# Attention of a two-layer transformer kernel: steps taken in pairs on TensorE, with four probability buffers in place of three

## What is computed

```python
def dense_block_attention(q, k, v):            # layer 0
    s = jnp.einsum("bqhgd,bkhd->bhgqk", qblk, k).astype(jnp.float32) * scale
    p = jax.nn.softmax(s, axis=-1).astype(v.dtype)
    return jnp.einsum("bhgqk,bkhd->bqhgd", p, v)

def window_sink_attention(q, k, v, kc, vc, sink):   # layer 1
    s_loc = jnp.where(valid, s_loc, -jnp.inf)  # |i - j| <= WINDOW
    p = jax.nn.softmax(jnp.concatenate([s_loc, s_ctx, s_sink], axis=-1), axis=-1)
    return einsum(p[..., :band], vb) + einsum(p[..., band:band + s_ctx_len], vc)
```

## Time and profile before

| what | value |
|---|---|
| median of 3 runs | 1504.19 us (1504.17 to 1505.51) |
| span of the profiled execution | 1502.7 us |
| TensorE (PE) busy | 1476.1 us, 98% |
| VectorE (DVE) busy | 989.5 us, 66% |
| ScalarE (ACT) busy | 706.6 us, 47% |
| GpSimd (POOL) busy | 667.3 us, 44% |
| mean granted TensorE clock | 0.999 |
| chain that ended last | PE 73% of the span, ACT 2%, issue 2%, DVE 1% |

### The profile page before, as it was taken

One profiled execution on the slowest core, in us unless ns is written; L12 is line 12 of the kernel. 1 busy time (PEld: TensorE's weight loads), 2 busy tenths in 40 slices (PEclk: granted clock), 3 DMA queues, 4 the chain that ended last, 5 costly groups with the idle time before them and its releaser, 6 DMA issues.

```text
span 1502.7 us, 26249 instructions
## 1 busy us (share of the span) xinstructions
PE 1476.1 (98%) x10198; PEld 1268.9 (84%) x10198; DVE 989.5 (66%) x1500; ACT 706.6 (47%) x1229; POOL 667.3 (44%) x447
## 2 busy tenths in 40 slices
PE   6999999999999999999999999999999999999997
PEld 4888874578999989999899999865579998999997
DVE  5899877579778556476667655766634655456464
ACT  4645326762733424334243544355536454445365
POOL 0031026602656334353435433355645756556463
PEclk9999999999999999999999999999999999999999
DMA  9532110045224142244546211200012423224222
GB/s 374 215 129 99 44 43 1 2 174 184 93 90 149 64 138 93 64 163 150 186 139 216 94 59 57 74 26 1 1 57 99 126 71 127 85 84 142 93 91 84
DMA packets 51674, 157.04 MB, mean 105 GB/s; under 512 B 5568, under 2 KB 13120, under 8 KB 50016
## 3 DMA queue, kind: packets, MB, share of 16 engines
q1 hardware_dynamic: 51120, 155.17, 30.0%
q0 software_dynamic: 432, 0.20, 0.1%
HBM read 153.38 MB, written 2.10 MB: 103 GB/s over the span
## 4 chain that ended last, share of the span: by engine, by line
PE 73%; ACT 2%; issue 2%; DVE 1%; POOL 0%; DVEq 0%; ACTq 0%
PE psum L3449 31%; PE psum L3476 13%; PE psum L3482 7%; PE psum L2862 6%; PE psum L3408 4%; PE psum L3134 3%; PE psum L3421 2%; PE psum L2938 2%; PE psum L3102 1%; PE psum L3032 1%; DVE product L1924 1%; PE psum L3119 1%; PE psum L3104 1%; PE psum L3106 1%; PE psum L3108 1%
## 5 line engine op out<-in xcount | busy, mean ns | idle before, releaser
L1181 POOL TENSOR_TENSOR flow<-fraw,fhi 128x512 fp32r<-128x512 f32 x168 | 232.8, 1405 | 100.2 <-ACT fhi L1629 90.7
L1629 ACT ACTIVATE fhi<-fraw 128x512 fp32r<-128x512 f32 (+1 forms) x272 | 163.3, 614 | 164.6 <-DMA fraw<-weights_dram 103.1
L3476 PE MATMUL psum<-gated,fhi 128*128 128x512 f32 (+1 forms) x1032 | 217.7, 355 | 0.0
L2862 PE MATMUL psum<-act,whi 128*128 128x512 f32 (+1 forms) x1008 | 215.5, 332 | 0.1
L1187 POOL TENSOR_TENSOR flow<-fraw,fhi 128x512 fp32r<-128x512 f32 (+1 forms) x96 | 125.9, 1331 | 180.5 <-ACT fhi L1629 179.9
L3476 PEld LDWEIGHTS psum<-gated,fhi 128*128 128x128 f32 x1032 | 169.2, 188 | 28.8 <-issue 0.3
L3449 PE MATMUL psum<-tlo,fhi 128*128 128x384 f32 (+1 forms) x608 | 187.9, 309 | 0.0
L3449 PE MATMUL psum<-thi,fhi 128*128 128x384 f32 (+1 forms) x608 | 187.8, 309 | 0.0
L2862 PEld LDWEIGHTS psum<-act,whi 128*128 128x128 f32 x1008 | 154.0, 189 | 20.8 <-issue 2.3
L2565 DVE SCALAR_TENSOR_TENSOR xT<-psum,mod,xT 128x512 f32<-128x512 f32 (+1 forms) x141 | 87.5, 654 | 95.8 <-PE psum L3482 95.8
L3449 PE MATMUL psum<-bhi,fhi 128*128 128x384 f32 (+1 forms) x456 | 140.6, 308 | 0.1
(11 more groups left out here) (293 smaller groups left out, 3340.4 us busy)
## 6 DMA issues: line engine op xcount, KB each, us to landing
fraw<-weights_dram SPq DMA_DIRECT2D x88, 512.0 KB, 3.8
adr_late<-adat_dram SPq DMA_DIRECT2D x49, 512.0 KB, 3.6
raw<-weights_dram SPq DMA_DIRECT2D x44, 512.0 KB, 3.4
fraw<-weights_dram SPq DMA_DIRECT2D x64, 256.0 KB, 2.8
adr<-adat_dram SPq DMA_DIRECT2D x26, 512.0 KB, 4.6
ada_w<-ada_dram SPq DMA_DIRECT2D x8, 1024.0 KB, 13.9
fraw<-weights_dram SPq DMA_DIRECT2D x32, 192.0 KB, 2.5
xT<-x_in_dram SPq DMA_DIRECT2D x3, 1024.0 KB, 16.8
```

Source lines behind the costliest of these rows:

```text
L1181: nc.gpsimd.tensor_tensor(low_piece(L, j, x), weight_piece(L, j, x), high_piece(L, j, x).bitcast(F32), ALU.subtract).then_inc(sem("f_lo"), 1)
L1629: A(high_piece(L, j, x)[:, 0:cols], source, ACT.Copy).then_inc(sem("f_hi"), 1)
L2862: last = MM(out_[:, o:o + t1 - t0], w_, a_[:, t0:t1], start=k == order[0] and j == 0, stop=k == order[-1] and j == 2)
L3476: MM(ps, wh_, a_[:, t0:t1], start=k == 0 and i == 0, stop=False)
```

## The change

TensorE takes two steps at a time: the scores of the next two steps, then the values of this step and the next. A piece of maxima stands before the two scores and another behind them. Sums, `rows` and the work of ACT move behind pairs; the first pair of scores stands ahead of the loop. `probT` becomes four separate buffers, the fourth of them in the place of the rope tables (`O_CON`), so the fourth exponential waits for the last rope. The pieces of layer 1 change their order and their places; the last piece of unit 1, now masked, is made in the last projection block. In layer 0 the first scores wait for both last projection blocks, and `rows(0, 1)` stands ahead of the loop.

```diff
-NPT = 3
+NPT = 4
...
-            units.append(dict(j=j, q0=0, nq=NX, slots=3, pieces=[far[0], ends, near[0], near[1], far[1]],
+            units.append(dict(j=j, q0=0, nq=NX, slots=3, pieces=[far[0], near[0], ends, far[1], near[1]],
...
 def pieces_beside(layer, i, a):
-    units = UNITS[layer]
+    n = len(UNITS[layer])
     if layer == 1:
-        n, p = (i + 1, 4) if a == 0 else (i + 2, a - 2)
-        return [], [(n, p)] if n < len(units) and p >= 0 and (n, p) != (1, 4) else []
+        p = {0: 0, 1: 1, 3: 2, 4: 3, 5: 4}.get(a)
+        return [(i + 2, p)] if p is not None and i + 2 < n else []
     if i % 2 == 0:
-        return [], [(i + 2, 0)] if a == 1 and i + 2 < len(units) else []
-    return [], [(i + 2, a)] if i + 2 < len(units) else []
-
-def rows_at(layer, i):
-    return layer
+        return [(i + 2 + a, 0)] if i + 2 < n else []
+    return [(i + 2, a + 1)] if i + 2 < n and a < 5 else []
+
+def rows_behind(layer, i, a):
+    n = len(UNITS[layer])
+    if layer == 1:
+        return i + 1 if a == 0 and i + 1 < n else None
+    u = i + 1 if a == 0 else i + 2
+    return u if i % 2 and a in (0, 4) and u < n else None
...
+                    if t == NPT - 1:
+                        act.wait_ge(*na("rope", L, 5 if L == 0 else 9))
...
+                def behind_short(i):
+                    if i + 1 < len(units):
+                        minus_top(0, i + 1)
+                    if i >= 2:
+                        out_high(i - 2)
+
+                def behind_long(i, a):
+                    heads = [(*divmod(i // 2, 2), *divmod(n, 2)) for n in range(4)]
+                    if a == 1:
+                        if i >= 2:
+                            inverse(i - 2)
+                        given_by_heads(*heads[0])
+                    if a == 3:
+                        if i >= 2:
+                            out_high(i - 2)
+                        given_by_heads(*heads[1])
+                        if i + 1 < len(units):
+                            minus_top(0, i + 1)
+                        inverse(i - 1)
+                        given_by_heads(*heads[2])
+                    if a == 5:
+                        given_by_heads(*heads[3])
+
+                def behind_windowed(i, a):
+                    if a == 1 and queries_at(1, i) is not None:
+                        q_high(1, queries_at(1, i))
+                    if a == 3:
+                        if i + 1 < len(units):
+                            minus_top(1, i + 1)
+                        if i >= 1:
+                            inverse(i - 1)
+                    if a == 5:
+                        if i + 1 < len(units):
+                            sink_share(1, i + 1)
+                        if i >= 1:
+                            out_high(i - 1)
...
                 for i, u in enumerate(units):
-                    for a in range(len(u["steps"])):
+                    for a in range(0, len(u["steps"]), 2):
                         exponential(i, a)
+                        exponential(i, a + 1)
...
                     for a in range(len(u["steps"])):
                         if a == 0 and i >= 1:
                             evacuate(i - 1)
-                        if L == 0 and short and a == 0 and i >= 2 or L == 0 and not short and a == 0 and i + 1 < len(units):
-                            top(0, i + 1)
-                        if L == 0 and short and a == 0 and i >= 2:
-                            outputs(i - 2)
-                        if L == 0 and not short and a == 1 and i >= 2:
+                        if L == 0 and i >= 2 and a == (0 if short else 1):
                             outputs(i - 2)
...
-                        if L == 0 and short and a == 1 and i >= 2:
+                        if L == 0 and i >= 2 and a == (1 if short else 3):
                             out_low(i - 2)
-                        for pieces in pieces_beside(L, i, a):
-                            taken(L, pieces, a)
+                        taken(L, pieces_beside(L, i, a))
...
-                        if a == 1 and i >= 1:
+                        if a == 2 and i >= 1 or a == 1 and short and i >= 1:
                             denominators(i - 1)
-                        if L == 1 and a == 4 and i >= 1:
+                        if L == 1 and a == 5 and i >= 1:
                             out_low(i - 1)
...
             def maxima(L, i, p):
...
-                if piece_banks(L, i, p)[0] == 0 and i >= 1:
-                    pe.wait_ge(*na("neg", L, i if L == 1 or i % 2 == 0 else i - 1))
+                if L == 1 and i >= 2:
+                    pe.wait_ge(*na("neg", 1, i - 1 if p < 2 else i))
...
             def rows(L, i):
...
+                if L == 1 and 1 <= i and i + 1 < len(U[1]):
+                    pe.wait_ge(*na("mx", 1, U[1][i + 1]["m0"] + 2))
-                if L == 0 and i == 1:
-                    pe.wait_ge(*ev(FIRST[("out", 0)] - 1))
-                if L == 0 and i > 2 and i % 2 == 0:
+                if L == 0 and i >= 1:
+                    pe.wait_ge(*na("neg", 0, i))
+                if L == 0 and i > 2:
                     pe.wait_ge(*na("fln", 0, i - 2))
...
             def attention(L):
...
-                if L == 0:
-                    pe.wait_ge(*ev(FIRST[("out", 0)] - 2))
-                else:
-                    for n in range(2):
-                        pe.wait_ge(*ev(FIRST[("out", 1)] - 2 + n))
+                for n in range(2):
+                    pe.wait_ge(*ev(FIRST[("out", L)] - 2 + n))
                 order = steps_of(L)
                 scores(0, 0)
-                scores_masked(0, 0)
-                for t, (i, a) in enumerate(order):
+                scores(0, 1)
+                if L == 0:
+                    rows(0, 1)
+                for t in range(0, len(order), 2):
+                    i, a = order[t]
+                    following = order[t + 2:t + 4]
+                    first, second = pieces_beside(L, i, a), pieces_beside(L, i, a + 1)
+                    for piece in first:
+                        maxima(L, *piece)
+                    for step in following:
+                        scores(*step)
+                    for piece in second:
+                        maxima(L, *piece)
+                    for step in following:
+                        scores_masked(*step)
+                    for piece in second:
+                        maxima_masked(L, *piece)
                     values(i, a)
+                    values(i, a + 1)
                     if a == 0 and i >= 1:
                         sums(i - 1)
-                    if a == rows_at(L, i) and i + 1 < len(units):
-                        rows(L, i + 1)
+                    if rows_behind(L, i, a) is not None:
+                        rows(L, rows_behind(L, i, a))
```

More of the change, by code:

```diff
@@ L490, in build @@
         bigr = [at(f"bigr{L}", [P, 2 * KT, T], (G, H)[L], F32R) for L in range(2)]
-        probT = [at(f"probT{L}", [P, NPT, 2, NX], (H, E + 3 * TILE)[L]) for L in range(2)]
+        O_PROBT = [[(H, E + 3 * TILE)[L] + 8 * NX * c for c in range(NPT - 1)] + [O_CON] for L in range(2)]
+        probT = [[at(f"probT{L}{c}", [P, 2, NX], O_PROBT[L][c]) for c in range(NPT)] for L in range(2)]
         O_OSB = [H + 4 * TILE, E + 7 * TILE]
@@ L603, in rows_bank @@
         def rows_bank(L, i):
-            if L == 0 and i > 0 and i % 2 == 0:
-                return bank(7)[:, NC_:2 * NC_]
-            return bank((7, 6)[L] if i == 0 else 0)
+            if L == 0:
+                return bank(7)[:, NC_:2 * NC_] if i > 0 and i % 2 == 0 else bank(7)
+            return bank(6 if i == 0 else 0)
         ident = con[:, CC_ID:CC_ID + P]
@@ L1143, in sums_of_probabilities @@
                             pool.wait_ge(*na("add", L, u["d0"] + a - 1))
[L1144 to L1145 removed]
+                        so_far = (probT[L][(t - 1) % NPT] if a == 1 else acc[L])[:, :, qa:qb]
+                        nc.gpsimd.tensor_tensor(acc[L][:, :, qa:qb], so_far, probT[L][t % NPT][:, :, qa:qb], ALU.add) \
                             .then_inc(sem("a_add"), 1)
@@ L1539, in attention @@
                 for i, u in enumerate(units):
-                    short = len(u["steps"]) < 4
-                    for a in range(len(u["steps"])):
+                    for a in range(0, len(u["steps"]), 2):
                         exponential(i, a)
-                        if L == 0 and not short and 2 <= a < 6:
-                            given_by_heads(*divmod(i // 2, 2), *divmod(a - 2, 2))
-                        if a == rows_at(L, i) + 1 and i + 1 < len(units):
-                            minus_top(L, i + 1)
-                        if L == 0 and short and a == 1 and i >= 2:
-                            out_high(i - 2)
-                        if L == 1 and a == 1 and queries_at(L, i) is not None:
-                            q_high(L, queries_at(L, i))
-                        if L == 1 and a == rows_at(L, i) + 2 and i + 1 < len(units):
-                            sink_share(L, i + 1)
```

(25 more changed lines are left out.)

16 lines of the change are left out of this document (3 added, 13 removed).

## The result

The changed kernel takes 1536.14 us (median of 4 runs, 1534.14 to 1538.31) against 1504.18 (4 runs, 1503.79 to 1505.51): ratio 1.0213, 95% interval 1.0199 to 1.0228. That is 32 us slower, where 12.4 was forecast and 1522 was the upper end of the range. The profiled execution took 1534.14 us, its span is 1532.4, 29.7 over the span before.

What follows compares the result with a forecast made beforehand. TensorE, busy 98% of the span, was taken to bound the kernel. With savings counted, layer 0's +4.5 and layer 1's +7.9 gave +12.4 on a median of 1504.19, so 1516.6 us, range 1503 to 1522.

Steps and rivals of the forecast that it cites:

- cheaper junctions: In both layers' attention, joining two steps saves TensorE 0.37 us in entering and leaving array shapes.
- GpSimd's loop in layer 0: Layer 0's long stretches are ruled by GpSimd's five adds, which need 13.1 to 13.3 us, so they hardly shrink.
- a maxima piece that waits for VectorE: In a layer 1 unit TensorE wants the second maxima piece at 9.9 us and gets it at 12.1.
- The saving: Pairing saves 5.9 us in layer 0 and 1.33 a unit, 10.6 in all, in layer 1: sum 16.5.
- I take the blocked one, as the row of the same instruction beside the same add has it: Layer 1's full units: `out_low` held at 1.72 us, `top` at 0.80, unit 15.75 against 14.83; four units +3.7.
- Should new waits of 2 to 4 us lower it, that would come on top, and no row here prices it: Both layers: a clock lowered from 2.4 GHz by new waits would add time; no size was given.
- The heads: Start of each layer's attention: layer 0's first sums end at 227.0, +4.5 us; layer 1's end later, +6.5.
- The last stretches: End of each layer's attention, held by GpSimd's four adds: 10.5 us against 10.65 in layer 0, no change in layer 1.
- Long stretches: Layer 0, from a short unit's sums to the next long one's: 13.1 to 13.3 us.
- Between: Layer 0, long unit's sums to short unit's: three stretches take 20.45 us, +0.8, with VectorE late by 2.5 and 1.0.
- Rival A: The cheaper junctions win and VectorE reaches the second maxima piece in time: 1488 us, faster; chance 0.12.
- Rival C: GpSimd's adds also hold `top`, `q_low` and `given` in both layers and exponentials come late: 1521 us; chance 0.15.

Runs made afterwards that it cites:

- e9_outputs: e7_tails with VectorE making `outputs` behind the second reduction and the outer maxima, not the third reduction, in layer 0's long units: 1499.57 us, ratio 0.9970.
- e2_half_adds: The changed kernel with GpSimd's adds of layer 1 over one of the two groups of heads alone, half the elements: 1520.81 us.
- e3_fill: The changed kernel with 16 more matmuls, results overwritten, in units 1 to 5 of layer 1 ahead of step 3's scores, where TensorE waited: 1532.38 us.
- e8_before_tails: The kernel before, single steps and three buffers, with the last unit's steps 3, 4 and 5 summed by TensorE: 1506.49 us, ratio 1.0018.
- e1_order: The changed kernel with VectorE making `top` and `out_low` behind the evacuation and the next unit's first reduction in layer 1: 1518.92 us, ratio 1.0095.
- e7_tails: e6_queue0 with the last unit's steps 3, 4 and 5 of each layer summed by TensorE, where it was step 5 alone: 1503.11 us.
- e6_queue0: e5_heads with both reductions ahead of `outputs`, outer maxima, `q_low` and `given` in VectorE's queue in layer 0's short units: 1509.69 us.
- e5_heads: e1_order with earlier first scores in layer 0, reordered first pair in layer 1, and GpSimd's first add there waiting for the last rotation: 1513.67 us, ratio 1.0060.
- e12_outlow: The changed kernel with only `out_low` moved behind the next unit's first reduction in layer 1: 1531.24 us.
- e11_top: The changed kernel with only `top` moved behind the next unit's first reduction in layer 1: 1517.93 us.

## Why the prediction was right or wrong, step by step

The direction was right, and the parts of the mechanism that were named were right in the main: cheaper junctions, GpSimd's loop in layer 0, and in layer 1 a maxima piece that waits for VectorE about once a unit. The size was wrong, +32 for +12.4. The profiled execution, the fastest of the four, is +29.7, so 17.3 us are to be explained there. Both layers went past their outer bounds: at its last sums layer 0 had lost 10.1 us (bound 7), layer 1 17.5 (bound 11). Two steps failed: the clock behind the waits was put at nothing (some 11 us), and the held instruction was the wrong one (3.4 us).

- **The saving.** Forecast 1.33 us a unit; TensorE's busy time in a full unit fell by 14.83 - 13.62 = 1.21. Over both layers, from the first scores to the last sums, the sum had 16.5; in e9_outputs, where the clock stays at 1.00, TensorE is busy 14.3 us less (5.0 and 9.2). Right, if a little high. Even with the order mended a unit of 14.3 us passes on only 0.5 of its 1.2.
- **"I take the blocked one, as the row of the same instruction beside the same add has it"**: this step failed. It held `out_low`, forecast at 1.72, and let `top` run free at 0.80. The chip did the reverse: `out_low` 0.68, `top` 1.94. What an add holds depends on where the add ends, and both instructions read two operands in SBUF. The waits came out at 2.7, the unit at 16.60 instead of 15.75. With `top` held as well, the prediction had worked out 16.3. The Trainium skill (GPSIMD Engine Reference, § 1 and Key points) states that GpSimd contends with VectorE instructions of two SBUF inputs; the measured hold of `top` agrees, and e2_half_adds shows it: without the add it is 0.88 again. The row of one instance was taken for a property of one instruction. Cost, at full clock: four units at 1.77 over before in place of 0.92, +3.4 us more.
- **"Should new waits of 2 to 4 us lower it, that would come on top, and no row here prices it"**: the term left out. It measured 3.0 and 1.6 us in the third and fourth full units (e3_fill takes them back), 2.7 between 245 and 252, and, with the last sums of a layer and the matmuls behind them, 1.1 in layer 0 and 2.5 in layer 1: some 11 us, more than half of the 17.3. It was named and set to zero, neither in the sum nor in the range. That is the larger failure.
- **The heads.** +4.5 forecast for layer 0, +5.4 measured, first sums ending 227.83 against 227.0. Layer 1: +7.3 against +6.5. The waits named are there: 1.7 us for the second eviction in layer 0, and in layer 1 2.3 for the reduction behind the rope, with 1.6 more for ScalarE's high part of the queries, which was not named (3.9 together, 4.35 forecast). That some 3.6 us of each head were work moved forward, due back at the end (busy 10.54 there before, 6.84 after; 7.99 and 4.41), was not seen.
- **The last stretches**, "10.5 against 10.65" and "0": right in size for the changed kernel (10.66 and 8.23), for a wrong reason; that is luck. They were TensorE's before (busy 10.54 of 10.65 and all of 7.99, and e8_before_tails) and became GpSimd's by the change.
- **Long stretches** at 13.1 to 13.3: measured 13.3 to 13.6. **Between**: 2.5 and 1.0 of waiting were taken with bounds 0 and 5 together; measured 3.14 and 1.17, that is 4.3, inside the bounds, and the clock on top: +4.4 for +0.8.
- **Rival A**, the gain, had as its point of decision that VectorE's chain falls under 4.0 us. e1_order puts that chain in order and gets 14.3 a unit. The gain was there once the order, the heads and the ends were mended (e9_outputs), and it was 5 us, not 16. **Rival C** named the right mechanism, `top` held in both layers (1.94 for 0.88, 1.28 for 0.42) and `q_low` in layer 1 (2.44 for 0.68), and was given 0.15; `q_low` and `given` of layer 0 ran free (0.94 and 0.88 at 241 to 243), the exponentials cost TensorE 0.8 us in all, and even so it stopped at 1521, for want of the clock.

One thing stays open: why the same wait is followed by the half rate in one place and not in another. That is so for the 2.7 us of the third and fourth full units and of the first two, and for the 2.0 us of e7_tails and e6_queue0. Each kernel has one profiled execution, so whether the places are the same in every execution isn't known either. And e5_heads changed both heads at once; no run parts them.

## What to carry to other kernels

When steps are joined on the bounding engine, list what the helper engines have queued ahead of the one result that the joined block waits for, and put that result's instruction first: `top`'s result was needed some 4 us later (1038.07) than the reduction queued behind it (1034.31). Price an idle gap on TensorE as its length and the half rate that may follow it; here 2.7 us of waiting cost up to 5.7. A held VectorE instruction is a property of the moment, so bound every one that reads two SBUF operands within reach of a GpSimd add, not the one whose row happens to show it.

## What the runs showed of the hardware

- A wait of 1.62 us was followed by the half rate in each of four units (e2_half_adds), one of 2.1 in every second (e12_outlow), one of 2.7 in two of four (the changed kernel), waits of 0.4 to 0.6 in none (e1_order, e11_top). In layer 0 a wait of 2.0 was followed by it in e7_tails and not in e6_queue0. In these executions a shorter wait was not a safer one.
- Matmuls that compute nothing, 1.4 us in a wait of 2.7, went with a granted clock of 1.00 in all four full units and made two of them 3.0 and 1.6 us shorter (e3_fill).
- The VectorE instruction that met GpSimd's adds was held past the add's end: 480 ns became 1575, and with its partner 0.88 us became 1.94; 256 columns of `outputs` took 1.98 where they took 0.41. Where the second operand lies in PSUM the same line is not held in any of its 8 instances: `outputs` of layer 1 takes 0.67 to 0.69 us, in the full units at a time when an add runs. The Trainium skill (SBUF — State Buffer, the section on its two separate sides) calls the shared port an exclusive lock for a whole instruction, against VectorE instructions with two SBUF inputs; by that it is the rest of the running add that counts. These rows agree: `top` met an add that ended at 1031.15, and its pair ended 0.68 us later; `out_low` of the kernel before ended 0.55 us behind its add.
